# The two gate products of a recurrent layer: from block-diagonal 128-row products to products of 64 rows

## The reference, cut to what matters

```python
uc, conv_new = _causal_conv(ux, conv_buf, p['conv_w'], p['conv_b'])
xb = x.reshape(B, T, LRU_BLOCKS, LRU_BW)            # 16 blocks of 64 features; x is uc
r_gate = sigmoid(einsum('btnc,ncd->btnd', xb, w_r) + b_r)
i_gate = sigmoid(einsum('btnc,ncd->btnd', xb, w_i) + b_i)
log_a = -LRU_C * r_gate * softplus(-lam_param)
a = exp(log_a)
u = sqrt(-expm1(2.0 * log_a)) * (i_gate * x)
# then h_t = a_t * h_(t-1) + u_t along the tokens
```

## Time and profile before

| | |
|---|---|
| median of 3 runs | 1968.31 us |
| the profiled execution | 1966.05 us, of which 1963.2 us from the first to the last instruction |
| TensorE busy | 1920.9 us (98%) |
| VectorE busy | 1277.0 us (65%) |
| ScalarE busy | 1061.2 us (54%) |
| GpSimd busy | 191.1 us (10%) |
| share of the chain that ended last | TensorE 87%, ScalarE 6%, VectorE 4% |
| mean granted TensorE clock | 0.996 of full speed |

### The profile page before, as it was taken

One profiled execution on the slowest core, in us unless ns is written; L12 is line 12 of the kernel. 1 busy time (PEld: TensorE's weight loads), 2 busy tenths in 40 slices (PEclk: granted clock), 3 DMA queues, 4 the chain that ended last, 5 costly groups with the idle time before them and its releaser, 6 DMA issues.

```text
span 1963.2 us, 37319 instructions
## 1 busy us (share of the span) xinstructions
PE 1920.9 (98%) x15214; PEld 1880.6 (96%) x15214; DVE 1277.0 (65%) x2334; ACT 1061.2 (54%) x1715; POOL 191.1 (10%) x242
## 2 busy tenths in 40 slices
PE   7999999999999999999999999999999999999997
PEld 7999999999998999999989999999999999999997
DVE  6667676765437766666667676767644388666666
ACT  6466666665236644444565757575732475444445
POOL 4312121100110000000041212120001000000000
PEclk9999999999999999999999999999999999999998
DMA  5323232222332332333313232322232323332221
GB/s 140 105 66 108 71 96 71 85 76 75 93 101 65 99 95 87 86 97 96 98 55 101 66 105 70 103 81 75 76 86 86 97 71 92 92 112 88 87 90 65
DMA packets 275709, 172.32 MB, mean 88 GB/s; under 512 B 7592, under 2 KB 271104, under 8 KB 275552
## 3 DMA queue, kind: packets, MB, share of 16 engines
q1 hardware_dynamic: 268000, 155.47, 27.0%
q0 software_dynamic: 7520, 14.59, 2.4%
q10 hardware_dynamic: 32, 0.04, 0.0%
HBM read 158.86 MB, written 11.21 MB: 87 GB/s over the span
## 4 chain that ended last, share of the span: by engine, by line
PE 87%; ACT 6%; DVE 4%; issue 2%; DMA 0%; SPq 0%; ACTq 0%; DVEq 0%
PE PJ L778 37%; PE PJ L1054 19%; PE PX L1115 13%; PE PJ L960 5%; PE PJ L790 3%; PE PX L989 2%; PE PX L1007 1%; PE PX L902 1%; PE PX L1027 1%; ACT w_hi L1286 1%; PE PX L790 1%; DVE T L1951 1%; PE PX L892 1%; DVE Y L1873 1%; DVE X L1876 1%
## 5 line engine op out<-in xcount | busy, mean ns | idle before, releaser
L1841 DVE TENSOR_TENSOR w_lo<-w_raw,w_hi 128x1024 fp32r<-128x1024 f32 x236 | 299.1, 1269 | 187.7 <-ACT w_hi L1286 186.6
L1286 ACT ACTIVATE w_hi<-w_raw 128x1024 fp32r<-128x1024 f32 x236 | 247.4, 1052 | 204.4 <-DMA w_raw<-in_w_down 120.3
L778 PE MATMUL PJ<-h_hi,w_hi 128*128 128x272 f32 x1536 | 328.4, 295 | 2.6 <-DVE T L1951 1.9
L778 PE MATMUL PJ<-h_hi,w_lo 128*128 128x272 f32 x1536 | 316.6, 288 | 0.0
L778 PE MATMUL PJ<-h_lo,w_hi 128*128 128x272 f32 x1536 | 315.9, 287 | 0.0
L778 PEld LDWEIGHTS PJ<-h_hi,w_hi 128*128 128x128 f32 x1536 | 239.5, 189 | 10.8 <-issue 8.8
L778 PEld LDWEIGHTS PJ<-h_lo,w_hi 128*128 128x128 f32 x1536 | 240.4, 188 | 0.0
L778 PEld LDWEIGHTS PJ<-h_hi,w_lo 128*128 128x128 f32 x1536 | 240.0, 189 | 0.0
L1054 PE MATMUL PJ<-u_hi,w_hi 128*128 128x272 f32 (+2 forms) x1016 | 215.8, 288 | 0.0
L1054 PE MATMUL PJ<-u_hi,w_lo 128*128 128x272 f32 (+2 forms) x1016 | 214.3, 288 | 0.0
L1054 PE MATMUL PJ<-u_lo,w_hi 128*128 128x272 f32 (+2 forms) x1016 | 213.9, 287 | 0.0
(11 more groups left out here) (409 smaller groups left out, 4760.9 us busy)
## 6 DMA issues: line engine op xcount, KB each, us to landing
w_raw<-in_w_in SPq DMA_DIRECT2D x110, 512.0 KB, 3.7
w_raw<-in_w_down SPq DMA_DIRECT2D x64, 512.0 KB, 3.6
w_raw<-in_w_up SPq DMA_DIRECT2D x62, 512.0 KB, 5.2
w_raw<-in_w_branch_attn SPq DMA_DIRECT2D x16, 512.0 KB, 3.6
w_raw<-in_w_branch_lru SPq DMA_DIRECT2D x16, 512.0 KB, 3.6
w_raw<-in_w_out SPq DMA_DIRECT2D x16, 512.0 KB, 3.6
out_prompt_k<-stage POOLq DMA_DIRECT2D x16, 256.0 KB, 2.8
out_prompt_v<-GA POOLq DMA_DIRECT2D x8, 512.0 KB, 5.6
```

The source lines that it names most:

```text
L778: mm = pe.matmul(PJ[:, buf, half, 0:HT], w[a], src[b][:, k0 + k, HT * half:HT * half + HT], start=first and k == 0 and a + b == 0, stop=en ...
L1286: act.activation(w_hi[:, n.hi, :, :], raw(n), ACT.Copy).then_inc(w_hi_ready, 1)
L1841: dve.tensor_tensor(low(n)[:], raw(n), w_hi[:, n.hi, :, :].bitcast(F32), ALU.subtract).then_inc(w_lo_ready, 1)
```

## The change

Before, `w_gate` held for each feature tile u and each gate j a 128 x 128 matrix with two 64 x 64 blocks on its diagonal and zeros elsewhere; a product used 128 rows. Now `w_gate` holds, for each u, the two gates of one block side by side: block b lies in rows 64b to 64b + 63, and its columns hold gate j at 64 times ((j + b) mod 2). There are still four products a call, but each has 64 rows and gives both gates of one block for one half of the tokens: block b goes into banks 2b and 2b + 1 of `PX`.

The outputs of the first gate stand in the rows of their features; those of the second stand in the other half of the rows. So ScalarE reads `PX` in halves of 64 rows, four instructions instead of two, and writes the second gate's across into the other half. Its bias has to stand in the rows that are read: a new small tile `bi_cross` keeps the second gate's bias with its halves exchanged, which VectorE fills once with four small copies at the start. `turn_k` now waits for one count of `lru_act` more, since banks 0 and 1 now hold block 0 of both gates. GpSimd's clearing of `w_gate` is gone; the eight DMAs a pair that fill it stay.

```diff
--- before.py
+++ after.py
@@ -152,7 +152,8 @@
         rl2 = sb("rl2", [P, 2, 2])
         rs = sb("rs", [P, NT])
         last = sb("last", [P, 2, 8, KT])
-        w_gate = sb("w_gate", [P, 2, 2, P])
+        w_gate = sb("w_gate", [P, 2, P])
+        bi_cross = sb("bi_cross", [P, 2, KT])
         T = sb("T", [P, 2, NT])
 
 
@@ -264,8 +265,8 @@
             sem, ("p_turned", "pt_hi_ready", "pt_lo_ready", "pv_done", "o_placed"))
         o_squared, o_ssq, o_rs, o_normed, o_hi_ready, o_lo_ready = map(
             sem, ("o_squared", "o_ssq", "o_rs", "o_normed", "o_hi_ready", "o_lo_ready"))
-        wg_zero, wg_landed, hist_ready, conv_first, conv_step, gates_done, lru_act, lru_step = map(
-            sem, ("wg_zero", "wg_landed", "hist_ready", "conv_first", "conv_step", "gates_done", "lru_act", "lru_step"))
+        bi_crossed, wg_landed, hist_ready, conv_first, conv_step, gates_done, lru_act, lru_step = map(
+            sem, ("bi_crossed", "wg_landed", "hist_ready", "conv_first", "conv_step", "gates_done", "lru_act", "lru_step"))
         gelu_done, ga_done, gb_done, l_hi_ready, l_lo_ready, b_scaled, m_hi_ready, m_lo_ready = map(
             sem, ("gelu_done", "ga_done", "gb_done", "l_hi_ready", "l_lo_ready", "b_scaled", "m_hi_ready", "m_lo_ready"))
         relu2_done, u_hi_ready, u_lo_ready, f_scaled = map(sem, ("relu2_done", "u_hi_ready", "u_lo_ready", "f_scaled"))
@@ -625,7 +626,6 @@
             for l in range(DEPTH):
                 pool.dma_start(rows[16 * l + R_CW:16 * l + R_CW + 4, :], A["conv_w"][l]).then_inc(small_landed, 16)
                 pool.dma_start(rows[16 * l + R_SC:16 * l + R_SC + 3, :], A["state_conv"][l, 0]).then_inc(small_landed, 16)
-            pool.memset(w_gate[:], 0.0).then_inc(wg_zero, 1)
 
             for l in range(DEPTH):
                 for j, name in enumerate(("lambda_q1", "lambda_k1", "lambda_q2", "lambda_k2")):
@@ -636,13 +636,13 @@
             def load_gate_weights(l, p):
 
                 g = 4 * l + p
-                need(pool, wg_zero, 1)
                 need(pool, gates_done, 2 * g, first=p == 0)
                 own_wait(pool)
                 for u in range(2):
                     for j, name in enumerate(("w_rg", "w_ig")):
                         for b in range(2):
-                            pool.dma_start(w_gate[64 * b:64 * b + 64, u, j, 64 * b:64 * b + 64],
+                            at_ = 64 * ((j + b) % 2)
+                            pool.dma_start(w_gate[64 * b:64 * b + 64, u, at_:at_ + 64],
                                            A[name][l, 4 * p + 2 * u + b]).then_inc(wg_landed, 16)
 
             def load_past(l, p):
@@ -897,9 +897,10 @@
                 pe.wait_ge(wg_landed, 16 * 8 * (4 * l + p + 1))
                 pe.wait_ge(conv_step, 3 * g2 + 3)
                 need(pe, lru_act, 5 * g2, first=p + u == 0)
-                for j in range(2):
-                    for half in range(2):
-                        mm = pe.matmul(PX[:, 2 * j + half, 0:LH], w_gate[:, u, j, :], uc[:, LH * half:LH * half + LH], start=True, stop=True)
+                for half in range(2):
+                    for b in range(2):
+                        r = slice(64 * b, 64 * b + 64)
+                        mm = pe.matmul(PX[:, 2 * b + half, 0:LH], w_gate[r, u, :], uc[r, LH * half:LH * half + LH], start=True, stop=True)
                 mm.then_inc(gates_done, 1)
 
             def sub_ssq(l, p, u):
@@ -915,7 +916,7 @@
 
                 need(pe, k_staged, 2 * g + m, first=p + m == 0)
                 if p > 0:
-                    pe.wait_ge(lru_act, 10 * g - 9 + 5 * m)
+                    pe.wait_ge(lru_act, 10 * g - 8 + 5 * m)
                 for grp in range(5):
                     o = PX[:, 1, 0:P] if grp == 0 else PX[:, 0, P * (grp - 1):P * grp]
                     mm = pe.transpose(o, T[:, m % 2, cols(grp)], ident[:])
@@ -1497,9 +1498,14 @@
                 act.wait_ge(gates_done, g2 + 1)
                 need(act, lru_step, 12 * g2, first=p + u == 0)
                 need(act, pv_lo_ready, 4 * l + p + 2 if p < 3 else 0)
+                act.wait_ge(bi_crossed, DEPTH)
                 for j, t in enumerate((tr, ti)):
-                    act.activation(t[:].rearrange("p (a b) -> p a b", a=2), PX[:, 2 * j:2 * j + 2, 0:LH], ACT.Tanh, scale=0.5,
-                                   bias=gain(l, f, R_BR + j)).then_inc(lru_act, 1)
+                    for b in range(2):
+                        to, by = 64 * b, 64 * ((j + b) % 2)
+                        i = act.activation(t[to:to + 64, :].rearrange("p (a b) -> p a b", a=2), PX[by:by + 64, 2 * b:2 * b + 2, 0:LH],
+                                           ACT.Tanh, scale=0.5,
+                                           bias=bi_cross[by:by + 64, l, f:f + 1] if j else gain(l, f, R_BR)[by:by + 64, :])
+                    i.then_inc(lru_act, 1)
 
                 act.wait_ge(lru_act, 5 * g2 + 1)
                 act.activation(aa[:], tr[:], ACT.Exp, scale=gain(l, f, R_LAM), bias=gain(l, f, R_LAM)).then_inc(lru_act, 1)
@@ -2017,6 +2023,9 @@
 
             def first_bias():
 
+                for l in range(DEPTH):
+                    dve.tensor_copy(bi_cross[0:64, l, :], par[64:P, :, 16 * l + R_BI])
+                    dve.tensor_copy(bi_cross[64:P, l, :], par[0:64, :, 16 * l + R_BI]).then_inc(bi_crossed, 1)
                 dve.tensor_scalar(bias_s[:, 0, :], bias_s[:, 1, :], -0.5 / SCALE, None, ALU.mult)
                 dve.tensor_scalar(bias_p[:, 0, :], bias_p[:, 1, :], -0.5 / SCALE, None, ALU.mult)
                 dve.tensor_scalar(bias_s[:, 1, :], bias_s[:, 1, :], -0.25 / SCALE, None, ALU.mult).then_inc(bias_ready, 1)
```

## The result

The changed kernel takes 2007.47 us (median of its runs, 2007.02 to 2008.58), the kernel before 1967.76 beside it: a ratio of 1.0205, with a 95% interval of 1.0191 to 1.0219. It is 40 us slower; the forecast was 20 us slower, and the time lies outside its range of 1976 to 1996. The profiled execution has a span of 2005.7 us.

What follows compares the result with a forecast made beforehand. The prediction took a just-in-time chain through ScalarE and VectorE to bound the kernel. Delays ahead of tile 6 (13.7), at pair 3's `sub_ssq` (4.8) and clock falls (3.5) made 22.0 us on 1966.05: 1988, range 1976 to 1996.

Steps and rivals of the forecast that it cites:

- What bounds the kernel: Whole kernel: TensorE is 98% busy only because a ScalarE and VectorE chain is just in time, about 0.25 us slack.
- ScalarE's term: Tanh of the gates: four half-row instructions instead of two put 1.20 us more ahead of `aa` per call, bounds 0.60 to 1.70.
- the six places: Ahead of tile 6, pairs 1 to 3 of both layers: TensorE starts 2.29 us later each, 13.7 us in all.
- pair 3: At TensorE's `sub_ssq`, which needs both tanh: 2.40 us later, twice, 4.8 us in all.
- The clock: TensorE's granted clock after new stalls at eight places: two falls, 3.5 us in all, bounds none and eight (14 us).
- the rival in which it falls at most of the stalls: TensorE's clock falls at most of the new stalls: 18.5 + 14 = 32 us, giving 1998; chance 8%.
- TensorE's term: Gate products: a call costs 1.46 us instead of 1.85, five pass times instead of eight; gain in time put at nothing.
- Small parts: VectorE's four bias copies, GpSimd's dropped clearing and ScalarE's wait for `bi_cross`: zero.
- half the rows take half the time: ScalarE's four tanh take as long as the two; time 1965, not slower; chance 5%.
- TensorE's gain arrives: Gate products' saving shows in the time since nothing waits: 6 to 9.9 us, giving 1956 to 1960; chance 3%.

Runs made afterwards that it cites:

- e3: Kernel before, products kept, with only the two tanh of each call split into two 64-row instructions in place; 1998.56 us, ratio 1.0163.
- e1: Changed kernel with 960 bytes left free behind `bi_cross`, so all later tiles stand at their old addresses; 1997.03 us, ratio 1.0155.
- e5: Changed kernel at the old addresses, 64-row products kept, but with the two whole 128-row ACTIVATEs of the kernel before; 1966.79 us, ratio 0.9995.
- e10: Kernel before with the tanh split by rows in the calls u = 0 alone; 1981.71 us, ratio 1.0074.
- e12: Kernel before with the tanh of every call split by columns, four of all rows and half the columns; 1972.30 us, ratio 1.0027.
- e4: Kernel before with the tanh split four ways in turn: halves alternating, same half twice running, half columns, whole; 1982.72 us.
- e11: Kernel before with four half-row tanh in every call, ordered so the same rows come twice running; 1993.65 us, ratio 1.0138.
- e6: Changed kernel at the old addresses with the four 64-row tanh of a call in four orders in turn; 2000.70 us.

## Why the prediction was wrong in its size

The ratios split the loss: the half-row tanh alone 0.0163 (e3), everything else of the change at the old addresses -0.0008 (e1 less e3), the addresses 0.0050 (changed less e1); 0.0205, 32 - 2 + 10 = 40 us. Such differences add up whatever the cause; that the middle one is next to nothing is borne out by e5, which has it alone and measures -0.0005. The terms below, each by its own rows, come to 20 + 6.9 + 10 + at most 8.6 = 45.5 us, so the clock's share is less than its upper bound.

- **What bounds the kernel: right.** The time follows the chain through ScalarE and VectorE with 0.11 us of slack a place (e3, e10 to e12), and TensorE's 98% did not mean that its savings arrive (e5).
- **ScalarE's term: the step that failed.** "Two consecutive ones start 152.32 - 151.72 = 0.60 apart. So a call has 2 x 0.60 = 1.20 us more ahead of `aa`." The row was of two instructions on the same rows. The new ones change rows at each step and start 0.71 to 0.74 apart, and so does `aa` behind them: 1.72. The bounds, 0.60 to 1.70, just missed it; the upper one let only the two added instructions cost 0.84 each, where four at that price would have been 2.16. With 1.72, each of the six places loses 2 x 1.72 - 0.11 = 3.3 us instead of 2.29 (20 instead of 13.7), pair 3 twice 3.4 instead of 2.4 (6.9 instead of 4.8). In e3 tile 6 of the first pair starts at 164.47 instead of 161.15, 3.32 us later.
- **A term that was missing: addresses.** `w_gate` halves its room and `bi_cross` takes 64 bytes, so everything behind stands 960 bytes lower. The diff shows it; the sum gave it no line. It cost 10 us, in TensorE's busy time (1922.2 us in e1, 1934.5 in the changed kernel) and not in its waits (71 us of idle time in both).
- **The clock: probably too small.** New falls take up to 8.6 us by the windows, not 3.5: they came at both places of pair 3 and at both renewals of the norm, of which the earlier trace rows show the first at 1.00 with as much idle time (18 - 13.76 and 20 - 15.78, both 4.2 us). Set beside the kernel before, matmul by matmul, the two renewals add 1.4 and 1.5 us, and the two places of pair 3 add 5.4 and 4.9 us, of which 3.4 each are ScalarE's; what is left over holds a little of the slower pace as well. At none of the six places ahead of tile 6 does the clock fall, so the rival in which it falls at most of the stalls is out.
- **TensorE's term: right in its worth, too cautious in its size.** The call shown costs 1.33 us instead of 1.46. The rule of the Trainium skill ("TensorEngine Tiling (Array Packing)", "Theoretical Speedup", up to 2x) has its part: the eight passes of the call at 129.76 start in four pairs (129.76, 130.10, 130.33, 130.56), not the five pass times that were counted. By the rule 1.85 us would become 0.93, an estimate; measured are 1.33, since the first pair takes 0.33 and changing over comes ahead and behind.
- **Small parts.** Their zero is not told apart from the 0.0008 above, which is smaller than what these intervals can tell. The rivals in which half the rows take half the time and in which TensorE's gain arrives are out as well (0.71 us each; e5).

## What to carry to other kernels

Before a tile of all rows is split by rows, look whether consecutive instructions overlap only as long as the rows stay the same; a cost "per instruction" read where they stay the same is a lower bound. Where a change alters the size of one tile in a packed memory, count everything behind it as moved, and keep the old addresses (a gap will do) when the change itself is to be judged. An engine that is busy for 98% is not what bounds the time where it takes over, with 0.1 us to spare, from a chain through other engines.

## What the runs showed of the hardware

- ScalarE overlaps consecutive ACTIVATEs of 548 columns by about 0.10 us when both read and write the same rows (0.59 to 0.62 apart, 0.70 long; the kernel before, e4, e11), and not at all when the rows read and written change (0.71 to 0.74 apart, in every call of e3) or when, in all orders tried, one of two neighbours crosses from one half of the rows to the other (0.71 to 0.74, in all 16 calls of e6).
- TensorE's pace on 272-column passes depends on where the tiles stand: 798 to 802 matmuls in 100 us at full clock, with nothing else changed. For shifts of 32 to 192 bytes this kernel became 2 to 14 us slower, falls of the clock included.
- Whether the clock falls at a stretch of idle time is decided by little: around the renewal of the norm it stayed at 1.00 before and was 0.91 in e5, whose work there is the same. The kernel before itself was granted from 0.991 to 0.996 on average from one execution to the next.
- A fall of the clock of the same size (0.91 over 20 us) costs 1.4 us or nothing: nothing where a wait for another engine follows it (e5, 0.45 us late at 604 and at 612 us), 1.4 where it comes behind the last such wait (the changed kernel).
